# First expert's turn, order of passes, 16-bit biases and loads by choice in a two-block kernel on one core

## What is computed

```python
logits = xt @ w_router + b_router                 # 512 tokens, 32 experts
top_vals, top_idx = lax.top_k(logits, 4)
top_gates = softmax(top_vals)
# tokens sorted by expert, in blocks of 128; for each block of expert e:
gate = xb @ w_gate[e] + b_gate[e]
up   = xb @ w_up[e] + b_up[e]
gate = minimum(gate, 7.0);  up = clip(up, -7.0, 7.0)
glu  = gate * sigmoid(1.702 * gate)
y    = (glu * (up + 1.0)) @ w_down[e] + b_down[e]
out  = sum over a token's 4 choices of top_gate * y      # then x + out, rmsnorm
```

## Time and profile before

| | |
|---|---|
| median of 3 runs | 1892.3 us (1891.77 to 1894.94) |
| the profiled execution | 1894.84 us, its span 1893.5 us |
| PE busy | 1827.2 us, 96% |
| DVE busy | 1421.9 us, 75% |
| ACT busy | 1175.6 us, 62% |
| POOL busy | 194.1 us, 10% |

### The profile page before, as it was taken

One profiled execution on the slowest core, in us unless ns is written; L12 is line 12 of the kernel. 1 busy time (PEld: TensorE's weight loads), 2 busy tenths in 40 slices (PEclk: granted clock), 3 DMA queues, 4 the chain that ended last, 5 costly groups with the idle time before them and its releaser, 6 DMA issues.

```text
span 1893.5 us, 20799 instructions
## 1 busy us (share of the span) xinstructions
PE 1827.2 (96%) x8267; PEld 1459.0 (77%) x8267; DVE 1421.9 (75%) x1219; ACT 1175.6 (62%) x876; POOL 194.1 (10%) x127
## 2 busy tenths in 40 slices
PE   7999869999999999999999999999998999999998
PEld 5777757888888888888888888888874777778876
DVE  4476678989989989999998998998984524665342
ACT  4353456777777777777777777777772345664231
POOL 1311010111211211111121121111001000000000
PEclk9999979999999999999999999999998999999999
DMA  7311457999999999999999999999995322122221
GB/s 255 112 48 64 156 188 285 359 363 357 359 375 356 358 369 359 357 362 363 355 364 366 358 357 366 354 368 364 359 343 206 134 67 67 45 73 89 89 78 45
DMA packets 95042, 487.16 MB, mean 257 GB/s; under 512 B 13832, under 2 KB 15408, under 8 KB 44768
## 3 DMA queue, kind: packets, MB, share of 16 engines
q1 hardware_dynamic: 81120, 462.64, 65.7%
q0 software_dynamic: 9520, 17.13, 2.4%
q10 hardware_dynamic: 4304, 6.03, 1.0%
HBM read 481.56 MB, written 20.97 MB: 265 GB/s over the span
## 4 chain that ended last, share of the span: by engine, by line
PE 91%; DVE 5%; ACT 2%; DMA 1%; issue 1%; SPq 0%; DVEq 0%; ACTq 0%; POOLq 0%
PE PS L441 83%; PE PS L673 3%; DVE WL L1216 2%; PE PS L841 1%; PE PS L853 1%; PE PS L834 1%; ACT WH L906 1%; DMA ring<-in_w_in_dram 1%; DMA yk<-yd 0%; PE PS L551 0%; DMA yd<-ys,dst 0%; PE PS L473 0%; DVE X L1227 0%; DVE X L1530 0%; DVE X L1533 0%
## 5 line engine op out<-in xcount | busy, mean ns | idle before, releaser
L1216 DVE TENSOR_TENSOR WL<-ring,WH 128x2048 fp32r<-128x2048 f32 x428 | 967.8, 2287 | 272.7 <-ACT WH L906 272.5
L906 ACT ACTIVATE WH<-ring 128x2048 fp32r<-128x2048 f32 x428 | 816.8, 1917 | 387.5 <-PE PS L441 387.4
L441 PE MATMUL PS<-WH,xh 128*128 128x512 f32 x1024 | 326.8, 400 | 2.5 <-DVE xl L1472 2.5
L441 PE MATMUL PS<-WL,xh 128*128 128x512 f32 x1024 | 321.5, 395 | 0.0
L441 PE MATMUL PS<-WH,xl 128*128 128x512 f32 x1024 | 320.3, 394 | 0.0
L441 PEld LDWEIGHTS PS<-WL,xh 128*128 128x128 f32 x1024 | 193.1, 189 | 45.4
L441 PEld LDWEIGHTS PS<-WH,xl 128*128 128x128 f32 x1024 | 193.0, 188 | 45.5
L441 PEld LDWEIGHTS PS<-WH,xh 128*128 128x128 f32 x1024 | 188.9, 189 | 42.5 <-DVE xl L1472 2.9
L1755 POOL DMA_INDIRECT yd<-ys,dst x32 | 64.1, 2003 | 997.7 <-ACT ys L1067 997.7
L441 PE MATMUL PS<-WH,hh 128*128 128x512 f32 x512 | 163.2, 400 | 2.5 <-DVE hl L1472 2.5
L441 PE MATMUL PS<-WL,hh 128*128 128x512 f32 x512 | 160.3, 394 | 0.0
(11 more groups left out here) (341 smaller groups left out, 2166.8 us busy)
## 6 DMA issues: line engine op xcount, KB each, us to landing
ring<-in_w_gate_dram SPq DMA_DIRECT2D x128, 1024.0 KB, 7.1
ring<-in_w_up_dram SPq DMA_DIRECT2D x128, 1024.0 KB, 7.1
ring<-in_w_down_dram SPq DMA_DIRECT2D x128, 1024.0 KB, 8.2
ring<-in_w_in_dram SPq DMA_DIRECT2D x32, 1024.0 KB, 5.4
ring<-in_w_out_dram SPq DMA_DIRECT2D x8, 1024.0 KB, 5.0
yk<-yd SPq DMA_DIRECT2D x6, 1024.0 KB, 7.0
X<-in_x_dram SPq DMA_DIRECT2D x4, 512.0 KB, 9.7
h2d<-HV ACTq DMA_DIRECT2D x4, 512.0 KB, 2.9
```

Source lines behind the costliest of these rows:

```text
L441: return P.matmul(ps, a, b, start=start, stop=stop)
L906: A.activation(WH[buf[n]], ring[spot[n]], ACT.Copy).then_inc(s_hi, 1)
L1216: V.tensor_tensor(WL[buf[n]], ring[spot[n]], WH[buf[n]].bitcast(F32), SUB).then_inc(s_lo, 1)
```

## The change

**Biases.** `b3` and `sel96` become 16-bit (BF16). The three rows of partitions of `b3` now hold three parts of 16 bits each. ACT makes the first, DVE subtracts it (`r1`), ACT copies that to the second and to `bmid`, DVE subtracts again into `bst`, ACT copies that to the third. The clearing on DVE is gone, and DVE's and ACT's work on `b3` stands behind the logits, at the experts' start, ahead of the high and low part of piece 3 of the first expert. `sel96` takes 64 instead of 128 bytes on a partition, and everything that `reg` places lies 64 bytes lower.

```diff
     GtT = place("GtT", [32, 4, 128], F32)
-    sel96 = place("sel96", [96, 32], F32R)
+    sel96 = place("sel96", [96, 32], BF16)
     FC = place("FC", [128, 40], F32)
...
     e2 = reg("e2", [128, 4, E, K], F32, 24)
-    b3 = reg("b3", [96, 2, D], F32R, 44)
+    b3 = reg("b3", [96, 2, D], BF16, 44)
+    r1 = reg("r1", [32, 2, D], F32, 72.5)
+    bmid = reg("bmid", [32, 2, D], BF16, 26)
     bst = reg("bst", [32, 2, D], F32, 64.25)
...
     dc = reg("dc", [128, 4], F16, 61.75)
-    sc = reg("sc", [96, 1], F32R, 61.875)
+    sc = reg("sc", [96, 1], BF16, 61.875)
     vi = reg("vi", [128, 1], F32, 62)
...
                 S.wait_ge(s_cr, 1)
-            for k in (0, 1):
+            for k in range(K if j == 0 else 0):
+                S.dma_start(yk[0][k // 2][:, k % 2], yv[0][:, k]).then_inc(s_x[k], 16)
+            for k in (0, 1) if j else ():
                 S.dma_start(yk[j][k], yv[j][:, 2 * k:2 * k + 2]).then_inc(s_yk[j], 16)
...
-    def rows_by_columns(n, kc, b0, hi, lo):
+    def rows_by_columns(n, kc, b0, hi, lo, turned=0):
...
             kk = 2 * kc + k
-            for hf in range(2):
-                mm(PS[:, b0 + hf, :], hi[:, kk], wh[:, k, 512 * hf:512 * hf + 512], kk == 0, False)
-            for hf in range(2):
-                mm(PS[:, b0 + hf, :], hi[:, kk], wl[:, k, 512 * hf:512 * hf + 512], False, False)
+            for w in (wh, wl):
+                for hf in range(2):
+                    mm(PS[:, b0 + hf, :], hi[:, kk], w[:, k, 512 * hf:512 * hf + 512], kk == 0 and w is wh, False)
+        if turned:
+            P.wait_ge(s_tl, turned)
+        for k in range(2):
+            kk = 2 * kc + k
             for hf in range(2):
...
     def tensor_gate_up(e):
-        P.wait_ge(s_tl, t_rows[e] + 1)
+        P.wait_ge(s_th, t_rows[e] + 1)
         for p in range(8):
...
                     P.wait_ge((s_eg, s_eu)[which], e)
-            last = rows_by_columns(n_g[e] + p, kc, 2 * which, xh, xl)
+            last = rows_by_columns(n_g[e] + p, kc, 2 * which, xh, xl, 0 if p else t_rows[e] + 1)
             if kc == 3:
-                P.wait_ge(s_b3, 1)
+                P.wait_ge(s_bh, 3)
                 for hf in range(2):
...
             last.then_inc(s_mm, 1)
+            if p == 1 and e == 1:
+                tensor_turn_mid(0)
             if p == 4:
...
     def tensor_down(e):
-        P.wait_ge(s_tl, t_mid[e] + 1)
+        P.wait_ge(s_th, t_mid[e] + 1)
         if e:
...
         for p in range(4):
-            rows_by_columns(n_d[e] + p, p, 4, hh, hl).then_inc(s_mm, 1)
+            rows_by_columns(n_d[e] + p, p, 4, hh, hl, 0 if p else t_mid[e] + 1).then_inc(s_mm, 1)
...
                 tensor_down(e - 1)
-            if e < E:
+            if 0 < e < E:
                 tensor_turn_mid(e)
...
-        if j == 0:
-            P.wait_ge(s_spk, 1)
-            P.wait_ge(s_bst, 48)
-            P.wait_ge(s_eg, E)
-            P.wait_ge(s_eu, E)
-            P.wait_ge(s_ys, E)
-            P.wait_ge(s_tl, 2 * E)
+        P.wait_ge(s_spk, 1)
+        P.wait_ge(s_bst, 48)
+        P.wait_ge((s_eg, s_eu, s_ys, s_tl)[j], E if j < 3 else 2 * E)
         for hf in range(2):
...
         P.wait_ge(s_dg, j + 1)
-        P.wait_ge(s_yk[j], 32)
+        if j:
+            P.wait_ge(s_yk[j], 32)
         for k in range(K - 1):
+            if j == 0:
+                P.wait_ge(s_x[k], 32)
             for hf in range(2):
...
     def scalar_experts():
+        scalar_turn8(0, xh)
         A.wait_ge(s_b3, 1)
+        A.activation(b3[32:64], r1, ACT.Copy)
+        A.activation(bmid, r1, ACT.Copy).then_inc(s_bh, 1)
+        A.wait_ge(s_b3, 2)
+        A.activation(b3[64:96], bst, ACT.Copy).then_inc(s_bh, 1)
+        A.wait_ge(s_bh, 3)
         A.wait_ge(s_h2, 64)
         high(first + NX - 1)
-        scalar_turn8(0, xh)
         for e in range(E + 1):
...
         low(ahead(n_v))
-        for i in range(2):
+        for i in range(3):
             V.tensor_copy(sel96[32 * i:32 * i + 32], C[0:32, IDENT:IDENT + 32])
-        V.tensor_copy(sel96[64:96], C[64:96, IDENT:IDENT + 32])
         low(ahead(n_v + 1))
...
         low(first + NS - 1)
-        V.wait_ge(s_bh, 1)
-        V.memset(b3[64:96].bitcast(F32), 0.0)
-        V.tensor_tensor(b3[32:64], bst, b3[0:32].bitcast(F32), SUB).then_inc(s_b3, 1)
         V.wait_ge(s_lgt, 4)
...
         vector_further_count()
-        low(first + NX - 1)
+        V.wait_ge(s_bh, 1)
+        V.tensor_tensor(r1, bst, b3[0:32], SUB).then_inc(s_b3, 1)
         V.wait_ge(s_gk, 1)
...
         vector_turn8(0, xh, xl)
+        V.wait_ge(s_bh, 2)
+        V.tensor_tensor(bst, r1, bmid, SUB).then_inc(s_b3, 1)
+        low(first + NX - 1)
         for e in range(E + 1):
...
                 for p in range(8):
-                    low(ahead(n_g[e] + p))
+                    if e or p < 7:
+                        low(ahead(n_g[e] + p))
                     if p == 1 and e:
...
                 vector_turn8(t_mid[E - 1], hh, hl)
+            if e == 0:
+                vector_turn8(t_rows[1], xh, xl)
+                vector_up(0)
+                vector_glu(0)
+                low(ahead(n_g[0] + 7))
+                continue
             for p in range(4):
-                if e:
-                    low(ahead(n_d[e - 1] + p))
+                low(ahead(n_d[e - 1] + p))
                 if e < E and p == 0:
...
             i = j % 2
-            V.wait_ge(s_yk[j], 32)
+            if j:
+                V.wait_ge(s_yk[j], 32)
+            else:
+                V.wait_ge(s_x[K - 1], 32)
             V.wait_ge(s_br, j + 1)
```

## The result

| | before | changed |
|---|---|---|
| median, 6 runs each, side by side | 1894.7 us (1891.8 to 1896.5) | 1861.3 us (1858.9 to 1863.7) |
| ratio | | 0.9826, 95% interval 0.9811 to 0.9840 |
| span of the profiled execution | 1893.5 us | 1861.9 us |
| PE busy | 1827.2 us | 1802.1 us |

The change makes the kernel 1.7% faster, 33 us. 15 were forecast. The direction was right and the time lies inside the range of 1849 to 1891, but the size was taken at less than half: the measured time lies between the forecast (1877.5) and rival A (1852).

The account below looks back on a forecast made before the run. PE was taken as the bound, busy 96% of the span, so only its idle time and time per matmul count. Terms 0.3 + 8.0 + 1.3 + 2.8 + 2.4 = 14.8 us off 1892.3 gave 1877.5; range 1849 to 1891.

Parts of the forecast that it names:

- rival A: All matmuls: tiles a multiple of 128 bytes apart run faster, 18.4 us in experts plus 7 outside; 1852, chance 0.28.
- Step 1: Before the first expert: logits start 1.8 us earlier, waiting only for `xh` saves 1.4; together 3.2 us.
- Step 2: First expert: bias work delays pieces 3 and 4, PE waits 1.35 and about 1.3; 0.3 of the 3.2 us stays.
- Step 3: First to second expert: 6.3 us wait for `eu` shrinks to 1.1, slow transposes and cold pairs go; 8.0 us saved.
- The cover named for low(11): Second expert: low(11) ready at 286.5, wanted at 289.9; the load behind lands at 293.6, asked for about 293.2.
- Step 4: Expert pieces: the order of passes costs nothing; 64 bias pairs in 16 bits save 0 to 2.6 us, 1.3 taken.
- step 5: Last expert: PE starts at `hh` 1.4 us sooner, and no cold pairs saves 1.4 more; 2.8 us.
- step 6: Join: split `yk` loads let combine(0) wait only for DVE's first addition; 2.4 us, bounds 0 and 2.4.
- Rival C: All matmuls: the moving tile's place decides, WH3 and WH4 slow to 233.3 ns; 1898.8, chance 0.17.
- rival D: Cover gone: first expert loses 2 us, the clock falls at second and last expert, join gains nothing; 1886.4, chance 0.15.

Follow-up runs that it names:

- e5: Kernel before with three tiny tiles sharing one 32-byte slot, so all behind them lies 64 bytes lower, where the change puts it: 1871.7 us, ratio 0.9876.
- e8: Changed kernel with the work on `b3` moved early: DVE's first subtraction before the logits, the rest ahead of `xh`: 1857.2 us, ratio 0.9797.
- e6: Changed kernel with the first expert's turn back at its old place in PE's order, and DVE's order there with it: 1864.5 us, ratio 0.9847.
- e7: Changed kernel with the old order of passes and PE waiting for the low part of the turned tiles: 1863.9 us, ratio 0.9836.
- e12: Changed kernel with the join as before: `yk` in two 1 MB loads for the first 128 tokens, down biases waiting for all: 1860.6 us, ratio 0.9823.
- e10: Changed kernel with early bias work, logits moved into PE's idle time, and DVE's join additions between its low parts: 1852.5 us, ratio 0.9773.
- e2: Kernel before with 64 unused bytes behind `sel96`, moving tokens and WH3, WH4 up 64 bytes: 1896.0 us, ratio 1.0007.
- e9: Changed kernel with two groups of routing logits each moved ahead of a set of transposes, into PE's idle time: 1855.1 us, ratio 0.9789.

## Why the prediction was right, and where it was not

The stages of three profiled executions, in us, cut at the starts of PE's rows; e1 is the changed kernel without its placement:

| stage | before | e1 | changed | predicted for the parts |
|---|---|---|---|---|
| up to the first expert's first matmul | 253.1 | 254.6 | 253.4 | −3.2 |
| to the turn of the second expert's rows | 25.8 | 28.8 | 28.5 | +2.9 |
| to the last transposes of `eu` | 1136.1 | 1126.7 | 1111.0 | −9.3 |
| to combine(0) | 31.9 | 26.5 | 26.3 | −5.2 |
| to the end | 446.6 | 444.8 | 442.6 | 0 |

**Step 1 failed.** `xh` alone did give 1.36 us (2.47 to 1.11). The 1.84 for the logits did not come: PE had them ready not at 234.4 but at 237.5, since its transposes and the last two groups of logits ran at the low clock. The step took PE's own time in this stretch from one profile and held it fixed. In the profile of before the clock fell too, but only within the last two groups of logits (5.31 for what is twice 1.87 at the high level); in each of the thirteen other kernels it fell sooner, between 221 and 227 us, where it fell at 230.7 in the kernel before. With PE late, DVE's work on `b3` was hidden: in e5, which still has it, the counting matmuls come 39.0 us behind the first out-projection row, in the changed kernel 39.8.

**Step 2 was right.** 1.92 and 1.15 where 1.35 and 1.3 stood, 2.8 us given back where 2.9 stood, and e8 shows that they hang on that queue.

**Step 3 was right in its mechanism.** The wait, the slow transposes and the cold pairs are gone. Its size is 6.6 by e6 and not 8.0, since there the cold pairs behind the wait were fewer than two and not five. Against the kernel before, with its five, the stage gave 9.4 at the old addresses (e1) for steps 3 and 4, where 9.3 was forecast. The cover named for low(11) and the load behind it held: no bracket on a weight in the second expert.

**Step 4 was right.** A bias pair takes 0.45 us where it took 0.47, as these two rows of the changed kernel show, and that is 64 x 0.02 = 1.3, the middle that was taken.

```profile
343.93 0.61 PE L445 MATMUL PS<-b,sel 96*128 96x512 bf16 x2
344.38 1.11 PE L677 MATMUL PS<-C,xg 128*128 128x128 f32 x8
```

The fp32r matmuls around it fell to the same 0.45, so it has to be asked whether this is the 16 bits or the placement. e1 has 16-bit biases at the old addresses, e5 fp32r biases at the new ones:

```profile
672.91 0.61 PE L446 MATMUL PS<-b,sel 96*128 96x512 bf16 x2
673.35 1.11 PE L678 MATMUL PS<-C,xg 128*128 128x128 f32 x8
```

```profile
668.58 0.63 PE L440 MATMUL PS<-b,sel 96*128 96x512 f32 x2
669.05 1.11 PE L672 MATMUL PS<-C,xg 128*128 128x128 f32 x8
```

0.44 in e1 and 0.47 in e5: it is the 16 bits. Over a stretch of ten matmuls around each pair it is 21 to 25 ns between e7 and e5, which share addresses and order of passes, so 1.3 to 1.6 us for all 64. The 215.7 ns per matmul that the prediction cites from the Trainium skill (TensorE: Matmul & The Clock Gate, "Wait — 56ns, not 53.3ns?") was not seen here: in the changed kernel the two matmuls of a bias pair start 226.8 ns apart.

**Steps 5 and 6 were right**, in their sum (5.5 against 5.2) and in their shares. e12 has step 5 without step 6: from the last transposes of `eu` to combine(0) it takes 28.6 us where 31.9 stood, so step 5 gave 3.3 (2.8 forecast) and step 6 gave 2.2 (2.4 forecast). The first choice landed 3.9 us after its issue, as the step said, and combine(0) went on 0.05 us behind DVE's first addition. That addition is held by DVE's three low parts of the second block, which stand in front of it:

```profile
1411.39 6.69 DVE L1229 TENSOR_TENSOR WL<-ring,WH 128x2048 fp32r<-128x2048 f32 x3 [14.48 <-ACT WH L914]
1418.00 2.35 DVE L1542 TENSOR_TENSOR X<-PS,X 128x1024 f32<-128x1024 f32 x2
```

They stood there before as well, from 1436.55 on and up to the row. That is why down biases that start earlier do not bring the addition forward; e10, which moves the additions ahead of the low parts, does, and then PE waits for the load. The rule of the Trainium skill that the prediction cites against the halves (DMA: Bandwidth & Descriptors, "Measured") shows in part: from the first issue to the last landing, four halves took 8.6 us where e12's two whole loads took 7.6. But the term did not fall to 0, since combine(0) needs only the first half in order to start.

Without the placement the gain was 14.4 us by the medians (e1) against 14.8, and that this is so near is luck. The stages of the two profiled executions, before and e1, add up to only 12.1: step 1 promised 4.7 us more than came (3.5 in the changed kernel), and the part behind combine(0), to which no step gave anything, gained 1.8.

**The choice that failed** is the one among the cases. The forecast took the shifted addresses at zero with a chance of 0.40, and rival A at 18.4 + 7 with 0.28. e5 measured the placement at 23, of them 17.5 in the steady experts. That is the term that was missing. 33 is 14.4 and 19.2 by way of e1, or 23.0 and 10.4 by way of e5; the two ways differ by no more than the width of the runs. The rows for it stood in the earlier trace rows: two kinds of piece side by side with the same instructions and nobody waiting. Their only difference was where they lie, and the prediction's own line on the addresses said that this difference would vanish. Whoever has two classes in the trace and finds that the change merges them has no ground to give "as now" the largest chance; "stays as now" was the one outcome that needed a rule of its own. Rival A's rule itself was too wide (a multiple of 128; it is 256), and was right here only because the change brings 256. By its own rule e2 would have gained the same, and gained nothing. Rival C (the place of the moving tile decides) fell with the first timeline, rival D (the cover is gone) with steps 2, 3 and 5.

## What to carry to other kernels

When a diff changes the size of any tile, list what lies behind it and compare the addresses of the tiles that one matmul reads together; in this kernel 64 bytes were worth more than all the reordering. Give the clock in a stretch of short matmuls and waits a range of its own, as no single profile shows which level it will have. Of a wait that is to go, look at the row ahead of the releaser on its own engine: what holds it now holds it afterwards. And check a bracket's releaser by its own end: if it ended before the wait began, as in e12, another one held the engine, often a load.

## What the runs showed of the chip

An fp32r matmul of 512 columns took 227.6 ns on average where the stationary and the moving tile lie a multiple of 256 bytes apart in a partition, and 233.3 where they lie 64 or 320 apart (modulo 512), 232.4 to 232.9 at 384, 234.0 at 352, 229 to 230 at 192. Over this kernel that is 1.2% (e5). The slow pace outlasted its piece by about four matmuls. A pair of 16-bit matmuls of 96 rows and 512 columns cost 21 to 25 ns less than the same pair in fp32r at the same addresses (e7 against e5).

The granted clock fell in the logits of the routing with idle times of at most 0.74 us around (e9), and in e7 it held behind a wait of 2.92 us at the last expert, but fell behind one of 2.37 us at the second. How long PE stood just before did not decide it in these rows. What does was not found.
